# Recurrent heads of a hybrid decoder step: which engine spreads the sample values over their blocks

## The reference, cut to what matters

```python
G = jnp.cumsum(lc, axis=2)                     # log decay
o = einsum(A, v) + einsum(q * exp(G), S)       # A: causal scores with decay
S = exp(Gl)[..., None] * S + jnp.einsum('bhsd,bhse->bhde', kc * jnp.exp(Gl - G), vc)
```

## Time and profile before

| | us |
|---|---|
| median of three runs | 1333.36 |
| the profiled execution | 1332.62 |
| its span, first to last instruction | 1330.6 |
| TensorE matmul busy | 1310.1 (98%) |
| VectorE busy | 802.6 (60%) |
| ScalarE busy | 595.6 (45%) |
| GpSimd busy | 189.4 (14%) |

### The profile page before, as it was taken

How to read it: one execution, slowest core, us unless ns; L and a number is a source line. 1 busy time by engine, 2 the same in 40 slices (tenths; PEclk the granted TensorE clock), 3 DMA queues, 4 the chain that set the end, 5 groups by cost and what they waited for, 6 DMA issues and landing times.

```text
span 1330.6 us, 32854 instructions
## 1 busy us (share of the span) xinstructions
PE 1310.1 (98%) x13100; PEld 1279.3 (96%) x13100; DVE 802.6 (60%) x1457; ACT 595.6 (45%) x1207; POOL 189.4 (14%) x321
## 2 busy tenths in 40 slices
PE   9999999999999999999999999999999999999997
PEld 8998999999999999997999999999999999999996
DVE  6476576656655632238988888968565565552224
ACT  5367355333333322237666666646433333332231
POOL 0111121111111100000211111211111111120000
PEclk9999999999999999999999999999999999999999
DMA  8312221223222322212332323341122322332211
GB/s 292 116 48 65 83 94 55 90 93 94 80 83 90 124 88 88 81 53 84 115 112 97 97 97 101 95 130 62 52 92 95 93 81 81 98 122 89 89 41 68
DMA packets 39686, 123.24 MB, mean 93 GB/s; under 512 B 4232, under 2 KB 12168, under 8 KB 39496
## 3 DMA queue, kind: packets, MB, share of 16 engines
q1 hardware_dynamic: 35400, 111.92, 26.4%
q10 hardware_dynamic: 4048, 10.00, 2.3%
q0 software_dynamic: 176, 0.44, 0.1%
HBM read 113.78 MB, written 8.57 MB: 92 GB/s over the span
## 4 chain that ended last, share of the span: by engine, by line
PE 92%; DVE 4%; ACT 2%; issue 1%; DMA 0%; POOL 0%; DVEq 0%; ACTq 0%; SPq 0%
PE acc L449 85%; PE aux L753 1%; DVE w_lo L1371 1%; PE aux L781 1%; PE aux L606 1%; PE aux L737 0%; DVE x L1593 0%; PE aux L776 0%; DVE mix L1588 0%; PE aux L527 0%; DVE h_lo L1380 0%; PE aux L628 0%; PE aux L618 0%; DMA raw<-in_w_in_ab 0%; PE aux L545 0%
## 5 line engine op out<-in xcount | busy, mean ns | idle before, releaser
L1371 DVE TENSOR_TENSOR w_lo<-raw,w_hi 128x512 fp32r<-128x512 f32 (+1 forms) x372 | 305.4, 825 | 323.4 <-ACT w_hi L883 323.2
L449 PE MATMUL acc<-h_hi,w_hi 128*128 128x272 f32 x2208 | 474.5, 292 | 3.8 <-DVE h_lo L1380 2.5
L449 PE MATMUL acc<-h_hi,w_lo 128*128 128x272 f32 x2208 | 464.6, 288 | 0.0
L449 PE MATMUL acc<-h_lo,w_hi 128*128 128x272 f32 x2208 | 463.2, 288 | 0.0
L449 PEld LDWEIGHTS acc<-h_hi,w_hi 128*128 128x128 f32 x2208 | 349.5, 188 | 16.1 <-issue 7.6
L883 ACT CAST w_hi<-raw 128x512 fp32r<-128x512 f32 (+1 forms) x372 | 236.2, 641 | 268.4 <-PE acc L449 262.9
L449 PEld LDWEIGHTS acc<-h_lo,w_hi 128*128 128x128 f32 x2208 | 349.9, 188 | 0.2
L449 PEld LDWEIGHTS acc<-h_hi,w_lo 128*128 128x128 f32 x2208 | 348.0, 189 | 0.0
L449 PE MATMUL acc<-g_hi,w_hi 128*128 128x272 f32 x704 | 153.1, 288 | 0.0
L449 PE MATMUL acc<-g_hi,w_lo 128*128 128x272 f32 x704 | 153.0, 289 | 0.0
L449 PE MATMUL acc<-g_lo,w_hi 128*128 128x272 f32 x704 | 152.3, 288 | 0.0
(11 more groups left out here) (256 smaller groups left out, 1345.2 us busy)
## 6 DMA issues: line engine op xcount, KB each, us to landing
raw<-in_w_up SPq DMA_DIRECT2D x88, 512.0 KB, 3.6
raw<-in_w_down SPq DMA_DIRECT2D x32, 704.0 KB, 4.1
raw<-in_w_in_c SPq DMA_DIRECT2D x32, 512.0 KB, 3.6
raw<-in_w_in_ab SPq DMA_DIRECT2D x18, 512.0 KB, 3.8
raw<-in_w_out_ab SPq DMA_DIRECT2D x8, 512.0 KB, 3.6
S<-in_state ACTq DMA_DIRECT2D x8, 512.0 KB, 3.7
o_ss<-Snew ACTq DMA_DIRECT2D x8, 512.0 KB, 2.7
raw<-in_w_out_c SPq DMA_DIRECT2D x8, 512.0 KB, 3.6
```

What stands on the lines that cost most here:

```text
L449: mm = pe.matmul(acc[out][:, t, 0:H], w[slot][:, wc], mv[:, kk_, t * H:(t + 1) * H], start=start and k == 0 and q == 0, stop=stop and k == ...
L1371: dve.tensor_tensor(w_lo[slot][:, to], raw[n % 4][:, cols], w_hi[slot][:, to], ALU.subtract).then_inc(lo_ready, 1)
```

## The change

VectorE's spread in tick 1 goes. GpSimd's program calls `spread(cur)` at the end of each head's turn, after the product `qG`, for all eight heads. In front of it stands a wait until the two matmuls that read the previous contents of `vbd` are done. The call that handled head 7 alone, at the start of GpSimd's last turn, goes.

```diff
@@ VectorE, hgrn_tick @@
-                    if t == 1 and cur is not None:
-                        dve.wait_ge(C["v_lo"], prev + 1)
-                        v3 = v3_s[:].rearrange("p (a b) -> p a b", a=1).broadcast_to([3 * NB * TS, NB, P])
-                        dve.tensor_tensor(vbd[:], v3, own[:], ALU.mult).then_inc(C["vbd_ready"], 1)
@@ GpSimd, hgrn @@
             def hgrn(prev, cur):
                 if prev is not None:
-                    if cur is None:
-                        pool.wait_ge(C["us_done"], 2 * prev)
-                        spread(prev)
-
                     pool.wait_ge(C["sg_ready"], prev + 1)
...
                     pool.wait_ge(C["eG_ready"], cur + 1)
                     pool.tensor_tensor(qG[:], eG[:], qn[:], ALU.mult).then_inc(C["qG_ready"], 1)
+                    if prev is not None:
+                        pool.wait_ge(C["us_done"], 2 * prev + 2)
+                    spread(cur)
```

## The result

| | before | after |
|---|---|---|
| median, both timed beside each other | 1332.83 | 1335.97 |
| the profiled execution | 1332.62 | 1335.70 |
| its span | 1330.6 | 1333.7 |

The ratio of the medians is 1.0022, with a 95% interval from 1.0016 to 1.0029, from 16 runs of each: the change costs 3.1 us. Both profiled executions show the same 3.1, so their traces can be compared row by row.

The account below looks back on a forecast made before the run. TensorE was taken as the bound (92% of the chain). The terms 1.57 (head 1) + 0.13 (behind head 7) + 0 (gap) gave 1.70 us over 1333.36, so 1335.1 us, range 1332.9 to 1337.0.

Parts of the forecast that it names:

- within 0.2%: Outcome class for the whole kernel: measured time less than 0.2% (2.67 us) from before; chance 0.84.
- the unknown terms: Terms not fixed by the profile, in heads 1 and 7: total cost between 0.85 and 1.83 us, 1334.2 to 1335.2.
- the slower rival: "Each head stalls": heads 2 to 7 also wait for AT_s, some 0.3 us each, past 2.09 us delay; 1338.6 us; chance 0.10.
- The forecast mechanism: GpSimd's spread blocks VectorE's clamp, queue 1.60 us late, one TensorE wait of about 1.6 us in head 1; chance 0.70.
- heads 2 to 6 were to stay at 31.83: Sign that the forecast is right: the stretches of heads 2 to 6 keep their length of 31.83 us.
- What goes, worth 0: VectorE's seven spreads of 1212 ns, 8.5 us in sum: removing them brings nothing TensorE needs earlier, worth 0.
- All clamps at 2.04: Sign: all eight clamps of line 1860 take near 2.04 us beside GpSimd's spread, where head 0's took 0.44.
- Nothing stalls: Rival: the clamp gets the memory first, or enough of head 1's wait comes back; 1333.4 us; chance 0.12.
- Head 1, 1.57 of wait: From head 0 to head 1 VectorE has no idleness, so TensorE waits 1.57 us for AT_s, once.
- Nothing given back at the gap of head 1: TensorE's 0.72 us "issue" gap at 652.91 could return up to 0.72 us of head 1's wait; taken as 0.
- 0.59 us "is absorbed in the next head" in heads 2 to 6: After 0.93 us of VectorE idleness, 0.59 us of delay is left; covered for TensorE and absorbed in the next head.
- Behind head 7, 0.13 (0 to 0.26): At most 0.26 us of the leftover delay lengthens TensorE's 0.72 us AT_s wait behind head 7; middle 0.13 taken.

Follow-up runs that it names:

- e6: Changed kernel, GpSimd's spreads of heads 0 to 6 moved to its next turn, its sg product behind the scan; only head 7's spread beside the clamp: 1332.38 us, ratio 0.9994.
- e7: As e6, but with head 0's spread beside the clamp too, so clamps are blocked in heads 0 and 7: 1334.29 us, ratio 1.0011.
- e10: e5 with one more scan and one more clamp on VectorE in front of the clamp in all eight heads: 1336.08 us, ratio 1.0025.
- e5: Changed kernel, all eight GpSimd spreads moved to its next turn, its sg product behind the scan; no clamp blocked: 1331.23 us, ratio 0.9990.
- e2: Changed kernel, GpSimd's spreads moved to its next turn except head 7's, its sg product held until us_done: 1334.10 us, ratio 1.001.
- e3: As e2, but with head 0's spread beside the clamp too (heads 0 and 7): 1334.91 us, ratio 1.0017.
- e4: As e2, but with the spreads of heads 1 to 7 beside the clamp and only head 0's early: 1335.42 us, ratio 1.0023.
- e8: As e6, but with the spreads of heads 1 to 7 beside the clamp and only head 0's early: 1334.07 us, ratio 1.0009.

## Why the prediction was right, and where it was not

Forecast 1335.1 in a range of 1332.9 to 1337.0, measured 1335.97: in the range, and slower by 0.22% where I gave "within 0.2%" the most; the interval lies across that line. In part the nearness is luck. The 1335.1 stands on a median of three runs, 1333.36, and 16 runs of the same kernel gave 1332.83; on that the sum is 1334.5, and its own bounds for the unknown terms (0.85 to 1.83) end at 1334.7. The range held the result because it took in the near end of the slower rival. The forecast mechanism is there in its place, but one of its signs failed: heads 2 to 6 were to stay at 31.83. And the cost is 3.1 where the sum said 1.7, and that has its reasons step by step.

- **What goes, worth 0.** Right: e6 lies at the time of before.
- **All clamps at 2.04.** Right in all eight (1.99 to 2.04), as is the 1.60 of delay behind them. "Nothing stalls" is out.
- **Head 1, 1.57 of wait.** It is 1.41: `AT_s` starts 1.63 late, at 644.02 where the sum made it 643.99, but TensorE's own work came 0.10 later and the restart took less. A small miss.
- **Nothing given back at the gap of head 1.** Off by 0.32: it shrank from 0.72 to 0.40, inside the stated bound. That the wait did it is not shown. With a wait like it the gap is 0.85 in e7 and 0.73 in e10, and without any wait 0.28 in e5; what sets it is open.
- **0.59 us "is absorbed in the next head" in heads 2 to 6.** This is the step that failed. I read the idle times of one head as free to swallow a delay again in every head, without asking whom they wait for. Head 4's row already had the answer: a slack of 0.33 at ScalarE's `w_hi`, against 0.59 left. I used that number for head 7 and not for the others. It costs 0.87 us in heads 2 to 7 (0.75 + 0.12), and the 0.1 of the first such wait in head 1, tick 5.
- **Behind head 7, 0.13 (0 to 0.26).** The same step again: 0.96 in place of 0.13. The bound held only one head's remainder. What arrives there has been carried on from all of them: VectorE is 3.14 us late and TensorE 2.17 (862.84 for 860.67), so 0.97 is VectorE's own lag.
- **The slower rival.** It had "each head stalls", at 0.3 us a head, from a delay of 2.09. The kind was right; place and price were not. TensorE is stopped in tick 5, at line 806, and not at `AT_s`, and no second blocked operation was needed. The point from which it decides is what the idle times of one lap take in, which is 1.01 + 0.33 (0.44 measured in head 4: 3.28 at `L1852` to 2.84): 1.3 to 1.5 us, and not the cover of TensorE.

So the sum with the measured sizes is 0.10 + (1.41 - 0.32 + 0.11) + 0.75 + 0.12 + 0.96 = 3.13. The 0.11 in the brackets is that wait in tick 5. The first 0.10 is a shift from before the heads that the traces show without a cause.

**A version that beats both** is e5: 1331.23, 1.7 us faster than before (the interval ends just under 1) and 4.7 faster than the change. It gains behind head 7, where before had its one blocked clamp: TensorE is 0.07 ahead of before at the end of head 7 and 1.25 ahead behind the sample products. TensorE's level products there, in e5, with no wait (before: 864.23 after 0.72):

```profile
863.39 0.33 PE L727 MATMUL aux<-lev 128*32 128x32 f32 x16
```

## What to carry to other kernels

Before you let an idle time absorb a delay, follow its releaser back. If that engine was itself fed by the delayed one, the idle time moves along with the delay, and only the waits for something outside the loop (here TensorE) take anything in. Add these up over one lap: a delay below the sum costs once, where there is no cover, and a delay above it costs in every iteration, and adds up until the last wait. When you put an instruction of GpSimd somewhere, what counts is which VectorE instruction comes beside it, and how much of GpSimd's is left at that point. Delaying the engine by plain extra work, without the suspect, is a cheap test of such a claim.

## What the runs showed of the hardware

- A product of GpSimd that had started first held up three kinds of VectorE instruction with all their operands outside TensorE's accumulators. The clamp took 2.04 for 0.44, a scaling 1.59 for 0.56, a scan with two inputs 1.73 for 1.29. Behind GpSimd's end each still ran for its own time less 0.14 to 0.26 (the clamp at 738.08 and the scaling 0.30, the scan 1.14), and `c_gn` with its accumulator operand stayed at 0.72 beside the same spread. The Trainium skill ("SBUF — State Buffer", section "Who interferes with whom") says of VectorE's modes that use both of its ports that whoever issues first holds the pair of memory ports that the two engines share for the whole instruction, while the other blocks fully. The rows agree in that VectorE stood until GpSimd was through; which mode it was in they don't show.
- A spread of 96x512 took 1.29 and stopped the clamp for some 0.50 (0.95 for 0.44), so the price is what is left of GpSimd's instruction when VectorE arrives, not its length.
- Behind the 1.68 us wait, the profiled execution of the change had its TensorE clock at the 1.2 GHz level for some 3.4 us. The stretches before, in and after it (columns as above, the clock is the third from the end):

```profile
865.00:868.00 3.00, 1.32 (x76) 1.14 (x77) 2.93 (x10) 2.62 (x6) 0.55 (x2) 1.00 0.20 27
868.00:872.00 4.00, 4.00 (x49) 3.97 (x39) 2.54 (x10) 0.63 (x4) 1.23 (x1) 0.57 0.31 117
872.00:876.00 4.00, 4.00 (x202) 3.43 (x202) 1.29 (x2) 0.69 (x2) 0.00 (x0) 1.00 0.01 4
```

  It did not count in the end. TensorE falls 0.91 further behind in it, from 3.14 (line 727) to 4.05 us (line 776) over before, but the 0.86 us gap before has in front of line 781 ("issue") is gone then, and behind it the lag is 3.13. e10 had a wait of 1.6 in the same place with the clock at 1.00 and a gap of 1.3 there: its lag over before is 3.16 at line 727 and 3.61 behind the gap. So its time comes close to the change's in part by chance. e2 had the dip after its wait there, and e3, e4 and e8, with waits of 1.7, had not. What decides it is open.
